# A key and value chunk moved into the opening of a two-block transformer kernel

## The reference

```python
m_lat = split(silu(c) @ ada_w[l] + ada_b[l], 6)        # shift, scale, gate, ...
m_ctx = split(silu(c_ctx) @ ada_w[l] + ada_b[l], 6)
h_lat = x_lat * (1 + m_lat[1]) + m_lat[0]
h_ctx = x_ctx * (1 + m_ctx[1]) + m_ctx[0]
qa, ka, va, qb, kb, vb = split(h @ w_in, [512, 640, 768, 1280, 1792])   # 2304 columns
qa, ka = rope(rms_norm(qa)), rope(rms_norm(ka))        # heads of 64; context without rope
ya = global_gqa(qa, ka, va); yb = neighbourhood_attention(qb, kb, vb)
...
```

## Time and profile before

| | us |
|---|---|
| median of 3 runs | 1574.95 |
| lowest and highest run | 1573.91, 1576.41 |
| span of the profiled execution | 1572.0 |
| TensorE busy in it | 1543.6 |
| VectorE busy in it | 1067.6 |
| ScalarE busy in it | 880.8 |

### The profile page before, as it was taken

How to read it: one execution, slowest core, us unless ns; L and a number is a source line. 1 busy time by engine, 2 the same in 40 slices (tenths; PEclk the granted TensorE clock), 3 DMA queues, 4 the chain that set the end, 5 groups by cost and what they waited for, 6 DMA issues and landing times.

```text
span 1572.0 us, 25520 instructions
## 1 busy us (share of the span) xinstructions
PE 1543.6 (98%) x9936; PEld 1319.7 (84%) x9936; DVE 1067.6 (68%) x1983; ACT 880.8 (56%) x1735; POOL 337.9 (21%) x340
## 2 busy tenths in 40 slices
PE   7999999999999999999999999999999999999998
PEld 4788778988887888887999988988888898888886
DVE  4743766666444525788787768777888668779874
ACT  2423873666652423568455555756766557567662
POOL 0201420355540000112011102242221014412210
PEclk9999999999999999999999999999999999999999
DMA  9766123345657224021545562424555534335551
GB/s 369 301 238 243 21 82 134 122 182 205 236 226 261 81 108 152 13 79 68 186 177 218 184 231 105 144 104 164 187 189 187 202 142 154 139 137 188 187 202 78
DMA packets 46951, 260.35 MB, mean 166 GB/s; under 512 B 11888, under 2 KB 13168, under 8 KB 18160
## 3 DMA queue, kind: packets, MB, share of 16 engines
q1 hardware_dynamic: 43952, 252.78, 43.7%
q0 software_dynamic: 1296, 4.72, 0.8%
q10 hardware_dynamic: 1584, 1.23, 0.2%
HBM read 257.64 MB, written 1.07 MB: 165 GB/s over the span
## 4 chain that ended last, share of the span: by engine, by line
PE 90%; DVE 4%; ACT 3%; DMA 2%; issue 1%; POOL 0%; SPq 0%; DVEq 0%; ACTq 0%
PE ps L512 22%; PE ps L513 21%; PE ps L514 21%; PE ps L764 8%; PE ps L765 5%; PE ps L667 2%; PE ps L689 2%; PE ps L676 2%; PE ps L528 2%; PE ps L1164 1%; PE ps L766 1%; DMA raw<-in_ada 1%; PE ps L575 1%; DMA raw<-in_ev_w_in 1%; PE ps L1191 1%
## 5 line engine op out<-in xcount | busy, mean ns | idle before, releaser
L1931 DVE TENSOR_TENSOR wl<-raw,wh 128x1024 fp32r<-128x1024 f32 (+2 forms) x304 | 357.5, 1217 | 249.9 <-ACT wh L1437 248.6
L1437 ACT CAST wh<-raw 128x1024 fp32r<-128x1024 f32 (+1 forms) x318 | 313.6, 1036 | 337.0 <-PE ps L514 302.3
L512 PE MATMUL ps<-xx,wh 128*128 128x256 f32 (+1 forms) x1006 | 328.1, 326 | 0.0
L514 PE MATMUL ps<-xx,wl 128*128 128x256 f32 (+1 forms) x1006 | 325.5, 324 | 0.0
L513 PE MATMUL ps<-xx,wh 128*128 128x256 f32 (+1 forms) x1006 | 325.5, 324 | 0.0
L512 PE MATMUL ps<-wh,xx 128*128 128x512 f32 (+2 forms) x780 | 285.9, 367 | 2.7 <-DVE xx L2356 1.2
L514 PE MATMUL ps<-wh,xx 128*128 128x512 f32 (+2 forms) x780 | 281.1, 360 | 0.0
L513 PE MATMUL ps<-wl,xx 128*128 128x512 f32 (+2 forms) x780 | 281.0, 360 | 0.0
L2302 DVE SCALAR_TENSOR_TENSOR arena<-ps,pv,arena 128x254 f32<-128x254 f32 (+2 forms) x352 | 192.9, 548 | 28.7 <-ACT arena L1637 19.3
L512 PEld LDWEIGHTS ps<-xx,wh 128*128 128x128 f32 x1006 | 189.9, 189 | 20.1 <-issue 4.0
L514 PEld LDWEIGHTS ps<-xx,wl 128*128 128x128 f32 x1006 | 189.9, 189 | 15.2
(11 more groups left out here) (242 smaller groups left out, 2234.9 us busy)
## 6 DMA issues: line engine op xcount, KB each, us to landing
raw<-in_ada SPq DMA_DIRECT2D x46, 1024.0 KB, 5.0
raw<-in_up SPq DMA_DIRECT2D x44, 1024.0 KB, 4.9
raw<-in_fin SPq DMA_DIRECT2D x44, 1024.0 KB, 4.8
raw<-in_down SPq DMA_DIRECT2D x22, 1024.0 KB, 4.8
raw<-in_fout SPq DMA_DIRECT2D x22, 1024.0 KB, 4.8
raw<-in_win SPq DMA_DIRECT2D x12, 1024.0 KB, 4.9
raw<-in_ev_w_in SPq DMA_DIRECT2D x9, 1024.0 KB, 7.4
raw<-in_wout SPq DMA_DIRECT2D x8, 1024.0 KB, 4.9
```

Of the source, the lines that this page charges most:

```text
L512: e.matmul(out, A[0], B[0], start=first, stop=False)
L514: return e.matmul(out, A[1], B[0], start=False, stop=last)
L1437: e.copy(hi_of(j)[:, a:b], raw_of(j)[:, a:b]).then_inc(*S.hi.up((j, half)))
L1931: e.tensor_tensor(lo_of(j)[:, a:b], raw_of(j)[:, a:b], hi_of(j)[:, a:b].bitcast(F), ALU.subtract).then_inc(*S.lo.up((j, half)))
```

## The change

The chunk of keys and values (`ev_w_in` 2) is loaded directly after `ev_w_in` 1, ahead of the last modulation pair, and split to a place of its own (`HOME`, 10240 and 12288). ScalarE and VectorE split it in the opening, between features 5 and 6. TensorE multiplies it feature by feature (`early_kv`), in banks 5 and 0, two token tiles to a bank, between the features of the queries; the last modulation pair stands between the keys' features 0, 1 and 2, behind feature 5 of the queries. The halves of features 1 and 2 stand in another order around the earlier pairs. Column products begin with bank 1 instead of 5, and the later modulation chunks are visited 2, 2, 3, 3, 2, 2, 2 at a time. The query and key tiles, the copies and the splits stand in another order on ScalarE and VectorE.

```diff
--- before.py
+++ after.py
@@ -76,7 +76,7 @@
 SUM_AT = {5: 0, 9: 1, 13: 2, 17: 3}
 SUM_FINISH = 18
 
-LATER = (2, 2, 2, 2, 2, 2, 2, 2)
+LATER = (2, 2, 3, 3, 2, 2, 2)
 
 SIGNALS = (
     "c", "cs", "sel", "pv", "bias", "par", "x", "xt0", "xt1", "xt2", "xt3", "rows", "rel", "out", "raw0", "raw1", "raw2", "raw3", "raw4", "raw5", "bt0", "bt1", "bt2", "bt3",
@@ -113,9 +113,9 @@
     def ev(*blocks):
         return [("ev_w_in", i, CH, "split") for i in blocks]
 
-    o = ada(0, 0, 4) + ev(0) + ada(0, 1, 5, 2, 6) + ev(1) + ada(0, 3, 7)
+    o = ada(0, 0, 4) + ev(0) + ada(0, 1, 5, 2, 6) + ev(1, 2) + ada(0, 3, 7)
     n = 8
-    for i, few in zip((3, 4, 2, 5, 6, 7), LATER):
+    for i, few in zip((3, 4, 5, 6, 7), LATER):
         o += ev(i) + ada(0, *range(n, n + few))
         n += few
     o += ada(0, *range(n, 24)) + ev(8)
@@ -212,7 +212,8 @@
 
     ORDER = chunk_order()
     J = {(name, i): j for j, (name, i, _, _) in enumerate(ORDER)}
-    SPLITS = [j for j, o in enumerate(ORDER) if o[3] == "split"]
+    KV = J["ev_w_in", 2]
+    SPLITS = [j for j, o in enumerate(ORDER) if o[3] == "split" and j != KV]
     SLOT = {J["ada0", 2]: NRAW, J["ada0", 6]: NRAW + 1}
     PREVIOUS, slot_of = {}, [None] * NRAW
     for j in range(len(ORDER)):
@@ -221,7 +222,7 @@
             PREVIOUS[j], slot_of[SLOT[j]] = slot_of[SLOT[j]], j
 
 
-    HOME = {J["down0", 10]: (0, 2048), J["od_w_in", 4]: (4608, 6656), J["ev_w_out", 3]: (7168, 9216), J["od_w_out", 3]: (7168, 9216)}
+    HOME = {KV: (10240, 12288), J["down0", 10]: (0, 2048), J["od_w_in", 4]: (4608, 6656), J["ev_w_out", 3]: (7168, 9216), J["od_w_out", 3]: (7168, 9216)}
     for l in range(2):
         HOME[J[f"up{l}", 0]] = (3072, 5120)
         for i in range(2):
@@ -265,6 +266,8 @@
 
 
     ROWS = [[6, 7], [2, 3], [0, 1], [4, 5]]
+
+    KV_BANK = (5, 0)
 
     def ada_bank(n):
         return 6 + n % 2
@@ -833,6 +836,19 @@
                 elif k == 3 and t == 3:
                     m.then_inc(*S.proj.up(("use", j)))
 
+        def early_kv(k, tiles=t4):
+
+            hv, lv = (v.rearrange("p (k n) -> p k n", k=8)[:, k, :] for v in (hi_of(KV), lo_of(KV)))
+            q.wait_ge(*S.hi.at((KV, k // 4)))
+            q.wait_ge(*low_done(KV, k // 4))
+            wait_feature("f0", k)
+            for t in tiles:
+                tk = slice(128 * t, 128 * t + 128)
+                out = ps[KV_BANK[t // 2]][:, 256 * (t % 2):256 * (t % 2) + 256]
+                m = mm3(out, (xh[:, k, tk], xl[:, k, tk]), (hv, lv), k == 0 and t % 2 == 0, k == 7 and t % 2 == 1)
+                if k == 7:
+                    m.then_inc(*S.proj.up(("kv", t), ("use", KV)))
+
         ada(0, 0)
         ada(0, 1)
         ada_finish(0)
@@ -843,26 +859,39 @@
             e.matmul(ps[0][32 * g:32 * g + 32, 0:256], silp[:, n % 8, 14:46], XT[:, n // 4 % 2, 0:256], start=True, stop=True)
         first(0)
         ada(1, 0)
+        first(1, (0, 1))
         ada(1, 1)
-        first(1, (0, 1))
+        first(1, (2,))
         ada_finish(1)
-        first(1, (2, 3))
+        first(1, (3,))
         ada(2, 0)
         first(2, (0, 1))
         ada(2, 1)
-        first(2, (2, 3))
+        first(2, (2,))
         ada_finish(2)
-        first(3)
+        first(2, (3,))
+        for k in (3, 4, 5):
+            first(k)
+        early_kv(0)
         ada(3, 0)
-        first(4, (0, 1))
+        early_kv(1)
         ada(3, 1)
-        first(4, (2, 3))
+        early_kv(2, (0, 1))
         ada_finish(3)
-        for k in (5, 6, 7):
+        early_kv(2, (2, 3))
+        for k in (3, 4, 5):
+            early_kv(k)
+        for k in (6, 7):
             first(k)
+        for k in (6, 7):
+            early_kv(k)
         for t in t4:
             BANK["q0", t] = BANK["q1", t] = bs[t]
+            BANK["kv", t] = KV_BANK[t // 2]
             free[bs[t]] = [(S.ea, ("qk", 2 * t)), (S.ea, ("qk", 2 * t + 1))]
+        for t in t2:
+            free[KV_BANK[t]] = [(S.ea, ("va", 2 * t)), (S.ea, ("va", 2 * t + 1))]
+        nb[0] = 0
         more = iter([(n, i) for n in (4, 5) for i in range(8)])
         count = iter(LATER)
 
@@ -874,10 +903,6 @@
         columns("ev_w_in", 3, 512, "qb0")
         ada_few()
         columns("ev_w_in", 4, 512, "qb1")
-        ada_few()
-        bs = tokens("ev_w_in", 2, "kv", t4, turns=False)
-        for t in t4:
-            free[bs[t]] = [(S.ea, ("va", t))]
         ada_few()
         columns("ev_w_in", 5, 512, "kb0")
         ada_few()
@@ -1473,7 +1498,7 @@
             q.wait_ge(*S.proj.at((bank, t)))
             if key[1] >= 2:
                 q.wait_ge(*S.vec.at((key[0], key[1] - 2)))
-            o = ps[BANK.get((bank, t), 0)][:, 256 if bank == "q1" else 0:]
+            o = ps[BANK.get((bank, t), 0)][:, 256 if bank == "q1" or bank == "kv" and t % 2 else 0:]
             e.copy(x, o[:, 0:64 * nh].rearrange("p (h d) -> p h d", h=nh)).then_inc(*S.ea.up(key))
             if norm:
                 q.wait_ge(*S.ea.last())
@@ -1681,7 +1706,8 @@
                 e.dma_start(rows[:, 128:144], T["od_sink"].partition_broadcast(128)).then_inc(*S.par.up("rows", by=16))
                 e.dma_start(lams, T["lam"].partition_broadcast(128)).then_inc(*S.par.up("rows", by=16))
             if k in (3, 5):
-                weights(SPLITS[k // 2])
+                weights(SPLITS[1] if k == 3 else KV)
+        weights(SPLITS[2])
         e.dma_start(pv[:, 96:NPV], T["pv"][:, 96:NPV]).then_inc(*S.pv.up("pv", by=16))
         q.wait_ge(*S.vec.at("angle"))
         e.activation(mr[:, 1, :, 16:32], mt[:, 0:2, 0:16], ACT.Sin).then_inc(*S.act.up("sin"))
@@ -1697,14 +1723,13 @@
         for tile in QK[2:4]:
             qk(tile)
         copies_qb(copy, 0)
+        for tile in QK[4:8]:
+            qk(tile)
         weights(after(J["ev_w_in", 3]))
-        for tile in QK[4:8]:
+        for tile in QK[8:12]:
             qk(tile)
         copies_qb(copy, 1)
         weights(after(J["ev_w_in", 4]))
-        for tile in QK[8:12]:
-            qk(tile)
-        weights(after(J["ev_w_in", 2]))
         copies_kb(copy, 0)
         weights(after(J["ev_w_in", 5]))
         copies_kb(copy, 1)
@@ -2373,6 +2398,7 @@
                 feature_low(k)
             if n == 2:
                 weights_half(SPLITS[1], 1)
+                weights(KV)
         weights(SPLITS[2])
         q.wait_ge(*S.par.at("rows"))
         e.tensor_copy(posf[:], posi).then_inc(*S.vec.up("posf"))
```

## The result

The changed kernel takes 1579.37 us (median of 13 runs, 1575.23 to 1584.84), the kernel before 1576.12 beside it (1573.91 to 1577.75): a ratio of 1.0021, 95% interval 1.0013 to 1.0030. That is 3.25 us slower, inside the forecast's range of 1573.0 to 1580.0, and 1.7 more than its +1.55. (The ratios in this document are the measurement's own; they can lie 0.0003 from the quotient of the two medians.) The profiled execution has a span of 1583.4 us, 11.4 above the profiled one of before. So the first question is how much of these 11.4 the other executions have too.

What follows compares the result with a forecast made beforehand. TensorE, 90% of the chain that ended last, was taken as the bound. Opening -1.35, waits +0.6 and +2.3 gave +1.55 us on the 1572.0 span, plus 2.95: 1576.5 us; own range 1574.5 to 1578.5, overall 1573.0 to 1580.0.

Steps and rivals of the forecast that it cites:

- The opening: TensorE up to the first column product: removing gaps gains 1.35 us, bounds 0.4 and 2.3.
- A: Stretch from TensorE's first matmul to the first column product, key and value block included; forecast 1.35 us shorter.
- The loads and splits: Opening: key and value chunk lands at 33.5, is split by 37.0, 1 us early; next weights reach ScalarE at 47.
- late weight chunk: Rival, chance 0.10: next weights land after 47, delaying the tile chain; 1577.9 us, at most 1581.4.
- The waits: TensorE waits for tile copies to empty banks: 0.6 us inside the first column product, 2.3 ahead of the second.
- 10.64: Time in us from the first tile copy to the fourth copy's end, used to place the first wait.
- No wait followed later: Second half of the second column product: no wait; third product: nothing, up to 1 us if a low part is late.
- B: Stretch from the first column product to a mark at 137.60 in the kernel before; forecast waits 0.6 and 2.3 lie here.
- the clock falls: Rival, chance 0.08: TensorE drops to 1.2 GHz in the 2.3 us wait, costing 1.7; 1578.2 us.
- the inference from 1.71: Full pace followed the 1.71 us gap ahead of the last modulation pair, taken as evidence against a clock fall.
- C: Stretch between marks at 137.60 and 218.07 in the kernel before, reaching into attention; forecast gave no change there.
- not borne out so far: Prediction's verdict on the skill's rule that short idles between matmul groups make the clock swing, citing the 1.71 us gap.

Runs made afterwards that it cites:

- a_again: The changed kernel, unaltered, profiled a second time; 1577.57 us against 1574.64 for the kernel before, ratio 1.0018.
- b_late_copy: The changed kernel with VectorE's copy of the first column product moved behind tiles 4 and 5; 1574.53 us, ratio 0.9996 to the kernel before.
- c_cover: The changed kernel with four modulation chunks instead of two between the first two column products, fewer later; 1574.24 us, ratio 0.9997 to the kernel before.
- j_order: The changed kernel with VectorE's next low part between fifth and sixth tile, a third modulation chunk between the first column products; 1574.67 us, ratio 0.9995.
- f_tile_first: The changed kernel with VectorE's low part of the next weights moved behind the third and fourth tile; 1576.54 us, ratio 1.0017 to the kernel before.
- l_after: The changed kernel, unaltered, once more on the chip of that call's other runs; 1577.34 us against 1575.09 for the kernel before, ratio 1.0017.
- g_both: The changed kernel with VectorE's next low part, then its column product copy, moved behind the sixth tile; 1579.33 us, ratio 1.0031 to the kernel before.
- k_order_f1: j_order with the kernel before's order at feature 1 restored in the opening; 1574.06 us, ratio 0.9991 to the kernel before.

## Why the prediction came out as it did

**The opening: right, and a little better than said.** The finish of the second pair is at 21.89 (21.7 was said), feature 2 resumes at 25.10 (24.9), feature 4 after a small wait at 32.67 (32.5); this execution starts 0.22 later than that of before (6.90 against 6.68). The pair's chunks come at 39.76 and 42.38 (39.6, 42.25), the last finish at 44.20 (44.15), the first column product at 59.97 (60.1). One sum in it is off by 0.1: from 32.5, two features of 2.83 end at 38.15 and not at 38.05. Over the twelve profiles with the change's opening A is 53.06 to 54.26, which spreads as much as the gain. But the spread lies ahead of feature 0, chiefly where thirteen matmuls (26 rows, L859) run at one of two paces; here they are in the changed kernel and then in a_again, the same program:

```profile
11.73 1.91 PE L859 MATMUL ps<-arena,silp 128*32 128x256 f32 x26
```

```profile
11.86 3.56 PE L859 MATMUL ps<-arena,silp 128*32 128x256 f32 x26
```

From the first matmul of feature 0 to the first column product all twelve take 45.37 to 45.49, and before takes 47.07 (14.38 to 49.76, and 11.69 for keys and values): a gain of 1.6 to 1.7, where 1.35 was said. Of before there is one profile. At the end of the run b_late_copy, c_cover and j_order, with most of the waits gone, come out at 0.1 to 0.4 faster and still have 0.6 to 1.0 of them.

**The loads and splits: right.** The chunk's copies start at 33.61 (33.5), nothing waits for it, and ScalarE reaches the next weights at 47.09 (47); their load took 9.1 and not 10.7, from 34.3 to 43.4, so there was no late weight chunk. ScalarE's timeline, against the earlier trace rows:

```profile
33.61 2.00 ACT L1462 CAST home<-raw 128x1024 fp32r<-128x1024 f32 x2 [1.69 <-DMA raw<-in_ev_w_in]
...
47.09 1.04 ACT L1462 CAST wh<-raw 128x1024 fp32r<-128x1024 f32 x1
...
65.68 0.37 ACT L1502 COPY arena<-ps 128x256 f32<-128x256 f32 x1 [4.36 <-DVE arena L2073]
...
75.59 0.37 ACT L1502 COPY arena<-ps 128x256 f32<-128x256 f32 x1 [5.20 <-DVE arena L2073]
```

**The waits: right, in place, cause and size.** The fourth tile copy ends at 66.05 (66.25) and TensorE waits 0.49 (0.6). The sixth ends at 75.96, TensorE waits 2.31 (2.3), and VectorE has idled 2.43 ahead of its copy of the first product's second half, which before came 3.7 after its product:

```profile
71.96 0.69 DVE L1944 TENSOR_SCALAR arena<-ps 128x512 f32<-128x512 f32 x1 [2.43 <-PE ps L517]
```

b_late_copy shows the cause of the second, f_tile_first that of the first (the next low part ahead of the third tile, a term that the prediction had inside its 10.64 without naming it). No wait followed later, as forecast.

**What failed: the clock's chance, and with it the sum.** The 1579.37 lies above the forecast's own range of 1574.5 to 1578.5; counted from the 1574.95 that the prediction had for before, it would be 1578.2 and inside. With the clock up, l_after's A + B is 1.27 above before's, near the +1.55: -1.7 for the opening, +2.8 for the two waits, and 0.2. But "the clock falls" was a rival with a chance of 0.08, and it came true in both other profiles of the changed kernel, and in f_tile_first and g_both. The step that failed is the inference from 1.71: full pace after a gap of 1.71 says that 1.71 does no harm, and nothing of 2.3, so 0.08 was too little. Its size was right: 1.7 was said, 1.5 to 1.6 measured in B. The rival's 1578.2 is +3.25, which is the median's +3.25 in the first comparison. That they are equal is in part luck, since the changed kernel's executions lose time in C too; in two other comparisons it came out at +2.9 and +2.25, as a mixture of executions with the fall and without would.

The section "A second HAM failure mode: psum-queue depth-cycling" of the Trainium skill's page "TensorE: Matmul & The Clock Gate" says that short idle times between groups of matmuls, as banks are cycled, can make the clock swing when they come often enough. Here one wait for a bank was enough: behind 2.31 us the clock fell in three of four profiles (0.5 for 3.41 us), and behind 1.45 it didn't. The 1.71 that the prediction held against that rule was a wait for a load and not for a bank, so "not borne out so far" was no answer to it.

**C was taken as fixed.** It isn't: 80.47 in before, a_again and g_both, up to 88.63 in others. In the changed kernel's first profile TensorE idled five times there, mostly without a releaser:

```profile
164.44 0.63 PE L679 MATMUL ps<-cs,arena 128*128 128x128 f32 x4 [0.79 <-issue]
171.15 0.67 PE L670 MATMUL ps<-arena 64*128 64x256 f32 x3 [0.92 <-issue]
...
175.72 1.59 PE L692 MATMUL ps<-arena 128*64 128x128 f32 x12 [1.20 <-issue]
```

The 6.83 us at 0.5 come on top, from 175.1. In the 18 us from 160 the queue that brings instructions (q8) took 2.3% of the DMA engines' time, in the 18 us from 157 of before 0.5%; whether an engine waited for it isn't shown. As the kernel before has a single profile, I can't say whether the change makes this commoner; its 33 runs beside j_order span 1573.4 to 1580.5, so it has executions that lose several us somewhere too.

## What to carry to other kernels

When work moves from one bank to banks that another chain must empty, follow the order of the engine that empties them: here one copy in VectorE's queue, which waits for TensorE itself, held back the tile that TensorE needed next, and moving that copy behind two tiles was worth 3 us. A new wait on the bounding engine costs its length and possibly the slower matmuls after it, so price a wait that is longer than any harmless one in the trace with the clock's term in the sum, not among the rivals. Before something is moved out of the way, ask when it is itself due: g_both lost 4.07 to the very step that it had pushed back.

## What the runs showed of the hardware

- The granted clock's answer to one and the same wait differs from execution to execution. After 2.31 us without work it fell to 0.5 for 3.41 us in three profiles (changed, a_again, f_tile_first) and stayed at 1.0 in one (l_after); after 4.07 it fell for 6.83; after 1.45 or less, or with the wait filled by other matmuls, it did not fall at this place in any of eight profiles.
- The pace at the kernel's start differs in the same way: the thirteen matmuls ahead of feature 0 took 1.91 to 1.92 us in ten profiles and 3.2 to 3.6 in four (a_again, b_late_copy, j_order, k_order_f1), and feature 0 came 0.7 to 1.1 us later for it. The Trainium skill's page "TensorE: Matmul & The Clock Gate", section "What's actually happening", calls the number of slow matmuls at a kernel's start variable from run to run. These profiles agree, and the changed kernel shows such a variation in mid-kernel as well.
- At the lower level a matmul of 512 columns starts every 0.427 us, at the higher every 0.227.
- One call for an f32 matmul of 256 columns on f32 data ran as two: ten calls are 20 rows, 4.24 us from the first start to the next product, 0.21 each.
